# Three LRU square roots moved one item later, and one weight split moved behind an exponential, in a hybrid attention and RG-LRU layer

## The reference, cut to what matters

```python
z = rms_norm(x) @ w_in                       # 1024 columns in, 3488 out
c_q, c_kv, k_r, u, gate_a, gate_b = split(z)
# branch A: low-rank attention, 16 heads, keys and queries normalised per head
# branch B: width-4 causal conv of u, then the RG-LRU recurrence:
r, i = sigmoid(u_c @ w_rg + b_rg), sigmoid(u_c @ w_ig + b_ig)
a = exp(-8 * r * softplus(-lam))
b = sqrt(-expm1(2 * log(a))) * (i * u_c)     # the "root"
h[t] = a[t] * h[t-1] + b[t]
x = x + (sigmoid(gate_a) * A + sigmoid(gate_b) * h) @ w_out
```

## Time and profile before

| | us |
|---|---|
| median of 3 runs | 858.15 (857.81 to 858.3) |
| the profiled execution's own time | 857.94 |
| its span, first to last instruction | 855.7 |
| PE busy | 839.1 (98%) |
| DVE busy | 574.7 (67%) |
| ACT busy | 362.5 (42%) |
| POOL busy | 200.6 (23%) |

### The profile page before, as it was taken

How to read it: one execution, slowest core, us unless ns; L and a number is a source line. 1 busy time by engine, 2 the same in 40 slices (tenths; PEclk the granted TensorE clock), 3 DMA queues, 4 the chain that set the end, 5 groups by cost and what they waited for, 6 DMA issues and landing times.

```text
span 855.7 us, 16818 instructions
## 1 busy us (share of the span) xinstructions
PE 839.1 (98%) x6548; PEld 804.8 (94%) x6548; DVE 574.7 (67%) x1056; ACT 362.5 (42%) x606; POOL 200.6 (23%) x228
## 2 busy tenths in 40 slices
PE   7999999999999999999999999999999999999998
PEld 7999898889999899877999999999999999999998
DVE  5596679877667676887656887888888886222121
ACT  6636869666645566566245222222212221222121
POOL 4022213202111121121140444333343245010000
PEclk9999999999999999999999999999999999999999
DMA  8432411131110200100223233232322323233321
GB/s 255 114 91 72 115 51 38 41 81 39 41 50 17 53 26 29 50 2 26 75 81 93 74 99 98 74 98 76 95 85 87 92 73 93 85 107 100 106 57 40
DMA packets 114466, 63.73 MB, mean 74 GB/s; under 512 B 7660, under 2 KB 112878, under 8 KB 114412
## 3 DMA queue, kind: packets, MB, share of 16 engines
q1 hardware_dynamic: 112428, 59.25, 24.4%
q0 software_dynamic: 1936, 3.70, 1.7%
q10 hardware_dynamic: 48, 0.02, 0.0%
HBM read 59.85 MB, written 2.70 MB: 73 GB/s over the span
## 4 chain that ended last, share of the span: by engine, by line
PE 88%; DVE 5%; ACT 4%; issue 2%; DMA 0%; SPq 0%; ACTq 0%; DVEq 0%
PE PS L1632 49%; PE PS L1785 9%; PE PS L1868 6%; PE PS L1840 4%; PE PS L1802 4%; PE PS L1678 3%; PE PS L1744 2%; PE PS L1822 2%; PE PS L2075 2%; PE PS L1776 2%; PE PS L1740 1%; PE PS L1707 1%; PE PS L1766 1%; PE PS L1644 1%; ACT w_hi L682 1%
## 5 line engine op out<-in xcount | busy, mean ns | idle before, releaser
L682 ACT ACTIVATE w_hi<-w_raw 128x1024 fp32r<-128x1024 f32 (+2 forms) x102 | 105.5, 1034 | 297.8 <-PE PS L1632 285.2
L1116 DVE TENSOR_TENSOR w_lo<-w_raw,w_hi 128x1024 fp32r<-128x1024 f32 (+2 forms) x102 | 128.2, 1257 | 106.7 <-ACT w_hi L682 106.7
L1632 PE MATMUL PS<-x2h,w_lo 128*128 128x272 f32 x704 | 145.7, 288 | 0.0
L1632 PE MATMUL PS<-x2h,w_hi 128*128 128x272 f32 x704 | 145.7, 288 | 0.0
L1632 PE MATMUL PS<-x2l,w_hi 128*128 128x272 f32 x704 | 145.1, 288 | 0.0
L1632 PEld LDWEIGHTS PS<-x2h,w_hi 128*128 128x128 f32 x704 | 110.8, 188 | 0.1
L1632 PEld LDWEIGHTS PS<-x2l,w_hi 128*128 128x128 f32 x704 | 110.6, 188 | 0.0
L1632 PEld LDWEIGHTS PS<-x2h,w_lo 128*128 128x128 f32 x704 | 109.9, 189 | 0.0
L643 POOL TENSOR_TENSOR uct<-uct 128x512 f32<-128x512 f32 x22 | 28.4, 1291 | 165.6 <-DVE uct L1585 165.6
L1632 PE MATMUL PS<-hh,w_hi 128*128 128x272 f32 x308 | 64.2, 289 | 0.0
L1632 PE MATMUL PS<-hh,w_lo 128*128 128x272 f32 x308 | 63.8, 288 | 0.0
(11 more groups left out here) (295 smaller groups left out, 1862.6 us busy)
## 6 DMA issues: line engine op xcount, KB each, us to landing
w_raw<-in_w_up_dram SPq DMA_DIRECT2D x44, 512.0 KB, 3.7
w_raw<-in_w_in_dram SPq DMA_DIRECT2D x24, 512.0 KB, 3.8
w_raw<-in_w_down_dram SPq DMA_DIRECT2D x16, 512.0 KB, 4.2
w_raw<-in_w_out_dram SPq DMA_DIRECT2D x8, 512.0 KB, 4.1
w_raw<-in_w_down_dram SPq DMA_DIRECT2D x8, 384.0 KB, 3.9
xnat<-in_x_prompt_dram SPq DMA_DIRECT2D x4, 512.0 KB, 5.0
w_raw<-in_w_in_dram SPq DMA_DIRECT2D x4, 416.0 KB, 6.3
wq<-in_w_q_b_dram SPq DMA_DIRECT2D x8, 192.0 KB, 2.6
```

The source lines that it names most:

```text
L682: nc.scalar.activation(hi[:, slot % 2, 0:n], raw[:, slot % 4, 0:n], ACT.Copy).then_inc(s_hi, 1)
L1116: tt(lo[:, slot % 2, 0:n], raw[:, slot % 4, 0:n], hi[:, slot % 2, 0:n].bitcast(F32), ALU.subtract).then_inc(s_lo, 1)
L1632: last = mm(joined_half(2 * rank, j), w[:, slot % 2, cols], x[:, k0 + k, j * HT:(j + 1) * HT], start=(k0 + k == 0 and first), stop=(k0 + k ...
```

## The change

Two calls on ACT are written in other places. `lru_mults(0, 3)` goes from the end of step `g == 5` to step `g == 6`, behind the two copies of the first keys. `split_item(I_IN + 12)` goes from in front of the key columns to behind `exps(0, 0)`. PE, DVE, POOL and SP keep their lists.

```diff
--- before.py
+++ after.py
@@ -1013,11 +1013,11 @@
                     lru_gates(g - 2)
                 if g == 4:
                     lru_exps(0, 3)
-                if g == 5:
-                    lru_mults(0, 3)
                 if 6 <= g < 9:
                     for u in range(2):
                         evacuate_kq(0, 2 * (g - 6) + u, 4 + u)
+                if g == 6:
+                    lru_mults(0, 3)
                 if g == 8:
                     squares_keys(0)
                     squares_queries(0)
@@ -1027,12 +1027,12 @@
                 evacuate_kq(1, u, 4 + u)
             for u in range(4, 6):
                 evacuate_kq(1, u, u - 4)
-            split_item(I_IN + 12)
             for v in (0, 1, 3):
                 columns_left(0, v, 4 + v)
             for u in range(3):
                 evacuate_v(0, u, (0, 1, 7)[u])
             exps(0, 0)
+            split_item(I_IN + 12)
             value_ones(0)
             squares_keys(1)
             for p in range(NP_):
```

## The result

The changed kernel takes 861.73 us (median of 5 executions, 860.83 to 862.46), the kernel before 858.15 (5 executions beside it, 857.81 to 858.48). The ratio is 1.0042, 95% interval 1.0028 to 1.0057: slower by about 3.6 us, outside what I called measurable (0.2%), and 0.23 us above my range. The direction was right, the size was not: I had 2.55.

The account below looks back on a forecast made before the run. PE, busy for 98% of the span, was taken as the bound. The moved roots' 1.5 us plus the moved split's 1.05 gave 2.55 over 857.94 or 858.15, called 860.6 us, range 859.0 to 861.5.

Parts of the forecast that it names:

- The first move, steps 1 to 5: ACT to DVE to PE, items 7 and 8: later roots and table load delay block 5's gates; keys start 1.5 us later.
- The second move: ACT, between first exponential and ones columns: the split has nothing to hide it there and costs 1.05 us (0.9 to 1.1).
- The table load: ACT's loads on the new path: 1.28 us each, without the skill page's further 1.38 us drain per switch.
- The clock falls: PE behind its new 3.2 us wait: clock drops from 2.4 to 1.2 GHz, 4.1 us more, 864.7 us; chance 0.06.

Follow-up runs that it names:

- e8: Kernel before with only `lru_mults(0, 3)` moved as in the change, plus ten identity matmuls in PE's wait for block 5's gates: 859.46 us, +1.47 over before.
- e3: Changed kernel plus ten identity matmuls, result unused, where PE waits for block 5's gates: 860.65 us, +2.51 over the kernel before.
- e4: Changed kernel plus a one-column sigmoid right behind the three roots, so the sigmoid table loads early: 859.29 us, +1.15 over the kernel before.
- e6: Kernel before with roots moved to step `g == 6` ahead of the key copies, split unmoved, one-column sigmoid behind the copies: 857.11 us, -0.88 over before.
- e1: Kernel before with only `lru_mults(0, 3)` moved as in the change, split left in place: 860.96 us, +2.82 over before.
- e7: Changed kernel with PE doing 42 instead of 30 matmuls of item 8 before breaking off for the keys: 859.06 us, +1.07 over the kernel before.
- e2: Kernel before with only `split_item(I_IN + 12)` moved as in the change, roots left in place: 858.86 us, +0.72 over before.

## Why the prediction was right and wrong

**The first move, steps 1 to 5: right.** With 0.75 added, block 4's second gate is read at 97.19 + 0.70 + 0.75 = 98.64 (I had 98.61); the keys begin at 98.70 without idle time (98.8); the first root ends at 103.36 (103.45); DVE waits 2.66 (2.6); the scan ends at 106.16 (106.25); item 7 is evacuated at 106.08 (106.25); the tap stands at 106.87 (107.05); the gate is read at 111.54 (111.7); PE waits 3.00 (3.2) and begins the keys 1.49 later (1.5). e8 gives +1.47 for it by time.

**The second move: right.** 0.95 by the profile, within 0.9 to 1.1, below the 1.05 taken. The values copies hid what the split gave back, as said.

**The table load: right.** In the changed kernel the load at 100.66 begins 0.02 us after the key copy has ended and the root begins 0.01 after the load. e3 measured 2.51 for the whole sum. The Trainium skill ("ScalarE: Activation LUTs", section "What ACT_TABLE_LOAD costs") adds a drain of 1.38 us to a switch, by which the sum would be 2.8 us larger, an estimate from that page. The trace agrees with the Trainium skill's 1.28 and not with its drain.

**The failing step: the rival "The clock falls".** The sum of 1.5 and 1.05 holds no term for the clock. The fall did not take the forecast's place, it came on top of it: 1.64 us by the rows. I gave it 0.06, against a wait that I had myself worked out as 3.2 us, because the earlier trace rows print a granted clock of 1.00 for the first 5.40 us, in which PE worked 0.26. That row was no evidence. The trace of the kernel before holds no entry of the granted clock ahead of 10.36 us, and a stretch without an entry is printed as 1.00. What the clock was there can be told from the pace of the matmuls. PE's forty transposes of L1644 follow that idle stretch. The busy time of two stretches among them, with the number of matmuls, reads:

```profile
5.38:8.50 3.12, 3.12 (x15) 3.12 (x16) 0.69 (x1) 0.60 (x1) 0.00 (x0) 1.00 1.02 408
10.30:12.10 1.80, 1.80 (x20) 1.55 (x18) 1.25 (x2) 1.16 (x2) 1.49 (x3) 1.00 1.10 368
```

PE is busy throughout and "1.00" is printed for both. Fifteen take 3.12 us, twenty a little later 1.80, but the last eight of the forty are smaller. Of the equal ones, those ahead of 10.36 start 0.21 us apart, those behind it 0.11. In all ten traces this step in pace falls where the entries of the clock begin, between 8.26 and 12.18 us. The same factor of two stands behind the 3.00 us wait, where the entries do say 0.51: the queries there start 0.32 us apart, and 0.16 in the kernel before. So PE came out of its idle start at the lower level, and the row that I held against the rival spoke for it. No experiment was made on these transposes; the reading rests on the factor and on the place of the step. The rule that I set aside for that row, of the Trainium skill ("TensorE: Matmul & The Clock Gate", section "What's actually happening"), that an idle PE is throttled to the lower level, is what the 0.51 behind the 3.00 us wait shows.

The price was off too. I let twice the first keys' 2.05 us run at half the pace, 4.1 us; the rows give 1.64, since the clock was full again by 115. A sum of 2.55 + 1.64 on 857.94 is 862.1, and the median of 861.73 lies between that and the forecast.

**What stays open.** Three of the five executions of the changed kernel have a mean granted clock of 0.998, like the profiled one; the two others have 1.000 and took 862.25 and 860.83, no less than the rest. A stretch without an entry counts as full in that mean, so 1.000 does not show that their clock stayed up, and no trace of them was kept. So the fall accounts for the profiled execution and, by e3 and e8, for 1.1 to 1.4 us of the medians, but a single execution's time is not told by its mean clock. Part of that is the spread ahead of the change: the row of item 6's evacuation from which I compare begins between 94.44 and 96.40 in the profiles of the nine altered kernels. That spread is made in the first 17 us. From PE's first product (L1678; L1679 and L1680 in e4 and e6) to that row it is 79.89 to 79.93 us in all ten profiles; ahead of it differ the start of the transposes (5.17 to 6.17) and the time until which they run at the slow pace. Why those differ is open.

## What to carry to other kernels

A step moved later on one engine is priced by what stands behind it on that engine and by which table it leaves loaded: here three roots that "only" moved past two copies carried a table load onto the path. When a sum produces a new wait of PE, look next at the matmuls behind it: a wait can cost more than its length, and filling it with work, real or idle, gives that part back. Before a printed clock is used as evidence, compare it with the pace of equal matmuls in that stretch or right behind it.

## What was not expected of the hardware

- One wait of PE of 3.0 us, in a span in which it is busy for 98%, was followed by a granted clock of 0.51 (e1: 0.55); waits of 1.5 and 1.6 us at the same place (e7, e4), and of 1.57 and 1.60 ahead of the first keys (the kernel before, e2), were not. Where between them it begins was not tried.
- A granted clock of 1.00 was printed for stretches of which the trace holds no entry, ahead of 8.26 to 12.18 us; there PE's transposes started 0.21 us apart, and 0.11 behind the first entry, in all ten traces.
- Ten matmuls of the identity in the wait kept the clock at 1.00 (e3) and made the kernel faster.
- ACT loads a table for an activation of one column as for any other, 1.28 us for the load and 0.20 for the column, so a load can be put into a wait that ACT has anyway (e4, e6).
